# First block's attention: high and low values side by side in one stationary tile, and the taps of each convolution chunk one step later

## What is computed

```python
h = rms_norm(x, mix_norm[l])
z = h @ w_in[l]
q = z[..., :Q_END].reshape(bsz, seq, N_Q_HEADS, HEAD_DIM)      # 8 heads of 64
k = z[..., Q_END:K_END].reshape(bsz, seq, N_KV_HEADS, HEAD_DIM) # 2 heads of 64
v = z[..., K_END:V_END].reshape(bsz, seq, N_KV_HEADS, HEAD_DIM)
attn_out = sliding_window_attention(q, k, v, attn_sink[l])      # blocks of 128, each sees itself and the one before
conv_out = short_conv(z[..., V_END:CB_END], z[..., CB_END:CC_END],
                      z[..., CC_END:CH_END], conv_w[l])         # b * conv3(c * h), causal, per channel
x = x + jnp.concatenate([attn_out, conv_out], axis=-1) @ w_out[l]
```

## Time and profile before

| | before |
|---|---|
| median of 3 runs | 2579.07 us (2578.69 to 2579.18) |
| profiled execution, span | 2577.6 us |
| PE busy | 2559.2 us, 99% |
| DVE busy | 1450.2 us, 56% |
| ACT busy | 947.2 us, 37% |
| POOL busy | 384.2 us, 15% |
| granted TensorE clock, mean | 0.999 of full |

### The profile page before, as it was taken

How to read it: one execution, slowest core, us unless ns; L and a number is a source line. 1 busy time by engine, 2 the same in 40 slices (tenths; PEclk the granted TensorE clock), 3 DMA queues, 4 the chain that set the end, 5 groups by cost and what they waited for, 6 DMA issues and landing times.

```text
span 2577.6 us, 32166 instructions
## 1 busy us (share of the span) xinstructions
PE 2559.2 (99%) x11610; PEld 2120.0 (82%) x11610; DVE 1450.2 (56%) x1735; ACT 947.2 (37%) x1381; POOL 384.2 (15%) x310
## 2 busy tenths in 40 slices
PE   8999999999999999999999999999999999999999
PEld 7888888888888888888888888888888888788887
DVE  7444347764443454443576644434999787642443
ACT  5222234432222232222354322223477534441332
POOL 4000111320001100001123100012177221100001
PEclk9999999999999999999999999999999999999999
DMA  5333332233333333333323333334233333233332
GB/s 160 98 98 94 97 87 83 82 100 96 98 96 96 102 91 97 98 92 98 96 66 91 98 97 98 94 96 126 73 81 76 123 90 112 76 107 97 98 98 82
DMA packets 487838, 247.21 MB, mean 96 GB/s; under 512 B 39874, under 2 KB 484551, under 8 KB 487495
## 3 DMA queue, kind: packets, MB, share of 16 engines
q1 hardware_dynamic: 487298, 245.75, 33.3%
q10 hardware_dynamic: 452, 0.32, 0.1%
HBM read 241.84 MB, written 4.19 MB: 95 GB/s over the span
## 4 chain that ended last, share of the span: by engine, by line
PE 95%; DVE 3%; ACT 1%; issue 0%; DMA 0%; POOL 0%; DVEq 0%; ACTq 0%
PE bank L669 15%; PE bank L668 15%; PE bank L670 15%; PE psT L668 10%; PE psT L669 10%; PE psT L670 10%; PE psS L668 4%; PE psS L669 4%; PE psS L670 4%; PE bank L684 1%; PE bank L677 1%; PE bank L680 0%; PE psT L778 0%; DVE wlo L1755 0%; PE bank L1083 0%; PE bank L1082 0%
## 5 line engine op out<-in xcount | busy, mean ns | idle before, releaser
L1755 DVE TENSOR_TENSOR wlo<-raw,whi 128x1024 fp32r<-128x1024 f32 x466 | 626.3, 1345 | 434.0 <-ACT whi L1285 417.4
L668 PE MATMUL bank<-xhi,whi 128*128 128x512 f32 x1656 | 648.1, 391 | 1.4 <-issue 1.4
L669 PE MATMUL bank<-xlo,whi 128*128 128x512 f32 x1656 | 644.7, 389 | 0.0
L670 PE MATMUL bank<-xhi,wlo 128*128 128x512 f32 x1656 | 644.6, 389 | 0.0
L1285 ACT ACTIVATE whi<-raw 128x1024 fp32r<-128x1024 f32 x463 | 485.3, 1050 | 340.5 <-PE psT L670 316.9
L668 PEld LDWEIGHTS bank<-xhi,whi 128*128 128x128 f32 x1656 | 311.0, 188 | 67.1 <-issue 2.9
L669 PEld LDWEIGHTS bank<-xlo,whi 128*128 128x128 f32 x1656 | 311.0, 188 | 64.7 <-issue 1.4
L670 PEld LDWEIGHTS bank<-xhi,wlo 128*128 128x128 f32 x1656 | 310.8, 188 | 64.9
L668 PE MATMUL psT<-hhi,whi 128*128 128x512 f32 x704 | 273.9, 389 | 0.0
L669 PE MATMUL psT<-hlo,whi 128*128 128x512 f32 x704 | 273.9, 389 | 0.0
L670 PE MATMUL psT<-hhi,wlo 128*128 128x512 f32 x704 | 273.9, 389 | 0.0
(11 more groups left out here) (516 smaller groups left out, 3457.5 us busy)
## 6 DMA issues: line engine op xcount, KB each, us to landing
raw<-in_ffn_wg SPq DMA_DIRECT2D x88, 512.0 KB
raw<-in_ffn_wu SPq DMA_DIRECT2D x88, 512.0 KB
raw<-in_ffn_wd SPq DMA_DIRECT2D x64, 512.0 KB
raw<-in_w_mlp SPq DMA_DIRECT2D x64, 512.0 KB
raw<-in_w_in SPq DMA_DIRECT2D x53, 512.0 KB
raw<-in_ffn_wd SPq DMA_DIRECT2D x32, 384.0 KB
raw<-in_w_in SPq DMA_DIRECT2D x24, 256.0 KB
raw<-in_w_out SPq DMA_DIRECT2D x11, 512.0 KB
```

The costliest lines, as they stand in the source:

```text
L668: pe.matmul(dest, a, rhs_hi(k), start=start and k == 0, stop=False)
L669: pe.matmul(dest, a, rhs_lo(k), start=False, stop=False)
L670: mm = pe.matmul(dest, b_, rhs_hi(k), start=False, stop=stop and k == tiles - 1)
L1755: dve.tensor_tensor(wlo[:, a:a + UNIT], raw[:, a:a + UNIT], whi[:, a:a + UNIT].bitcast(F32), ALU.subtract).then_inc(s_split, 1)
```

## The change

Three things change.

1. `vhi` and `vlo` become one tile `vst` in which each head's 64 high and 64 low columns of v lie side by side. With it as the stationary operand one matmul gives high v x p in rows 0 to 63 of `psO` and low v x p in rows 64 to 127. `pv` makes two matmuls for each key block in place of three (low v x low p comes along).
2. The attention output is the sum of the two halves of `psO`. ACT makes the high part of the first half alone; DVE makes the low part in two operations: first half minus high part into `olow1`, then plus second half.
3. DVE's two taps of chunk i, POOL's gate product and the high and low parts move one step of u later (taps at u = 3i + 4, parts at u = 3i + 5); for the last chunk they stay at u = 12. ACT's first tap stays.

```diff
--- before.py
+++ after.py
@@ -154,13 +154,14 @@
         khh = [sb(f"khh{g}", S, F32R) for g in range(2)]
         kll = [sb(f"kll{g}", S, F32R) for g in range(2)]
         half1 = [slice(0, HD), slice(HD, P)]
-        vhi = sb("vhi", S, F32R)
-        vlo = sb("vlo", S, F32R)
+        vst = sb("vst", 2 * S, F32R)
+        v_part = lambda e: vst[:, :].rearrange("p (n t d) -> p n t d", t=2, d=HD)[:, :, e, :]
         sc = [sb(f"sc{i}", 8 * P) for i in range(2)]
         pthi = sb("pthi", 8 * P, F32R)
         ptlo = sb("ptlo", 8 * P, F32R)
         upad = [sb(f"upad{i}", S + 8) for i in range(2)]
         cy = [sb(f"cy{i}", S) for i in range(2)]
+        olow1 = sb("olow1", S)
         assert at[0] <= top, (at[0] - top)
 
 
@@ -780,18 +781,20 @@
                 mm.then_inc(a_tt, 1)
 
             def pv(l, s):
-                blk = s // 2
+                blk, g = s // 2, s % 2
                 n = 1 if blk == 0 else 2
                 pe.wait_ge(a_th, l * STEPS1 + s + 1)
                 if s:
                     pe.wait_ge(a_ol, l * STEPS1 + s)
-                tiles = [(slice((blk - n + 1 + j) * P, (blk - n + 2 + j) * P), slice(j * 4 * P, (j + 1) * 4 * P)) for j in range(n)]
+                tiles = []
+                for j in range(n):
+                    v0 = (2 * (blk - n + 1 + j) + g) * P
+                    tiles.append((slice(v0, v0 + P), slice(j * 4 * P, (j + 1) * 4 * P)))
                 for j, (vs, ps) in enumerate(tiles):
-                    pe.matmul(psO[:, :], vhi[:, vs], pthi[:, ps], start=j == 0, stop=False)
-                    pe.matmul(psO[:, :], vlo[:, vs], pthi[:, ps], start=False, stop=False)
+                    pe.matmul(psO[:, :], vst[:, vs], pthi[:, ps], start=j == 0, stop=False)
                 pe.wait_ge(a_tl, l * STEPS1 + s + 1)
                 for j, (vs, ps) in enumerate(tiles):
-                    mm = pe.matmul(psO[:, :], vhi[:, vs], ptlo[:, ps], start=False, stop=j == n - 1)
+                    mm = pe.matmul(psO[:, :], vst[:, vs], ptlo[:, ps], start=False, stop=j == n - 1)
                 mm.then_inc(a_pv, 1)
 
             def mix(l, q, N):
@@ -1333,7 +1336,7 @@
                         c += 1
                     if i == 2:
                         act.wait_ge(s_vt, l + 1)
-                        act.activation(vhi[:, :], psT[:, 0:S], ACT.Copy).then_inc(s_vh, 1)
+                        act.activation(v_part(0), psT[:, 0:S].rearrange("p (n d) -> p n d", d=HD), ACT.Copy).then_inc(s_vh, 1)
                     act.wait_ge(s_qs, l * 5 + i + 1)
                     f = tmp[1 + i % 2]
                     if i == 0:
@@ -1354,7 +1357,7 @@
                         act.wait_ge(a_pv, l * STEPS1 + s + 1)
                         rows = slice(g * HD, (g + 1) * HD)
                         act.activation(yhi[rows, 0:4 * S].rearrange("p (c n) -> p c n", c=4)[:, :, blk * P:(blk + 1) * P],
-                                       psO[rows, :].rearrange("p (c n) -> p c n", c=4), ACT.Copy).then_inc(a_oh, 1)
+                                       psO[0:HD, :].rearrange("p (c n) -> p c n", c=4), ACT.Copy).then_inc(a_oh, 1)
                     if 0 <= u - 2 < STEPS1:
                         s = u - 2
                         n = 512 if s < 2 else 1024
@@ -1375,9 +1378,9 @@
                         act.wait_ge(c_u, l * CC + i + 1)
                         act.activation(cy[i % 2][:, :], upad[i % 2][:, 2:2 + S], ACT.Copy,
                                        scale=cw1[:, ds(l * (3 * CC) + 2 * CC + i, 1)]).then_inc(c_t2, 1)
-                    if (u % 3 == 1 and u >= 4) or u == 3 * CC:
-
-                        i = u // 3 - 1
+                    if (u % 3 == 2 and u >= 5) or u == 3 * CC:
+
+                        i = (u - 1) // 3 - (u < 3 * CC)
                         act.wait_ge(c_y, l * CC + i + 1)
                         act.activation(chunk(yhi, 4 + i), cy[i % 2][:, :], ACT.Copy).then_inc(c_yh, 1)
                 for m in range(KC):
@@ -1858,7 +1861,8 @@
                                              inv[:, :], ALU.mult, ALU.mult).then_inc(s_qs, 1)
                     if i == 2:
                         dve.wait_ge(s_vh, l + 1)
-                        dve.tensor_tensor(vlo[:, :], psT[:, 0:S], vhi[:, :].bitcast(F32), ALU.subtract).then_inc(s_vl, 1)
+                        dve.tensor_tensor(v_part(1), psT[:, 0:S].rearrange("p (n d) -> p n d", d=HD), v_part(0).bitcast(F32),
+                                          ALU.subtract).then_inc(s_vl, 1)
                     if i:
                         qk_low(l, i - 1)
                 for i in range(2):
@@ -1890,10 +1894,12 @@
                         dve.wait_ge(a_oh, l * STEPS1 + s + 1)
                         rows = slice(g * HD, (g + 1) * HD)
                         ys = slice(blk * P, (blk + 1) * P)
-                        dve.tensor_tensor(ylo[rows, 0:4 * S].rearrange("p (c n) -> p c n", c=4)[:, :, ys],
-                                          psO[rows, :].rearrange("p (c n) -> p c n", c=4),
-                                          yhi[rows, 0:4 * S].bitcast(F32).rearrange("p (c n) -> p c n", c=4)[:, :, ys],
-                                          ALU.subtract).then_inc(a_ol, 1)
+                        heads = lambda a: a.rearrange("p (c n) -> p c n", c=4)
+                        dve.tensor_tensor(heads(olow1[rows, :]), heads(psO[0:HD, :]), heads(yhi[rows, 0:4 * S].bitcast(F32))[:, :, ys],
+                                          ALU.subtract).then_inc(a_os, 1)
+                        dve.wait_ge(a_os, l * STEPS1 + s + 1)
+                        dve.tensor_tensor(heads(ylo[rows, 0:4 * S])[:, :, ys], heads(psO[HD:P, :]), heads(olow1[rows, :]),
+                                          ALU.add).then_inc(a_ol, 1)
                     if 0 <= u - 2 < STEPS1:
                         s = u - 2
                         n = 512 if s < 2 else 1024
@@ -1924,8 +1930,8 @@
                         c += 1
                     if 4 <= u + 1 < 3 * CC:
                         conv_part(u + 1, q + c)
-                    if u % 3 == 0 and u >= 3:
-                        i = u // 3 - 1
+                    if (u % 3 == 1 and u >= 4) or u == 3 * CC:
+                        i = (u - 1) // 3 - (u < 3 * CC)
                         y = cy[i % 2][:, :]
                         dve.wait_ge(c_t2, l * CC + i + 1)
                         dve.scalar_tensor_tensor(y, upad[i % 2][:, 1:1 + S], cw1[:, ds(l * (3 * CC) + CC + i, 1)], y,
@@ -2202,7 +2208,7 @@
                     rest = olow2[rows, :].rearrange("p (i n) -> p i n", n=P)
                     dve.tensor_tensor(rest, psO[0:HD, 0:2 * P].rearrange("p (i n) -> p i n", n=P),
                                       view(a2h).bitcast(F32), ALU.subtract).then_inc(a_os, 1)
-                    dve.wait_ge(a_os, r + 1)
+                    dve.wait_ge(a_os, L * STEPS1 + r + 1)
                     dve.tensor_tensor(view(a2l), psO[HD:P, 0:2 * P].rearrange("p (i n) -> p i n", n=P), rest,
                                       ALU.add).then_inc(b_ol, 1)
                 if s % 2 == 0 and h < H2:
```

## The result

| | before | changed |
|---|---|---|
| median | 2578.96 us (2578.69 to 2579.34, 21 runs) | 2583.97 us (2581.78 to 2585.82, 21 runs) |
| profiled execution, span | 2577.6 us | 2582.0 us |
| matmuls | 11610 | 11582 |

The account below looks back on a forecast made before the run. TensorE, busy 99% of the span, was taken as the bound, with DVE nearly full in the mixing stage. Per layer -3.17 + 1.7 + 2.5 = +1.0 us, +2.05 us for two layers: 2581.1 us, range 2575.3 to 2584.8.

Parts of the forecast that it names:

- Removed matmuls: Mixing stage on PE: 14 matmuls fewer a layer at 0.2267 us each, 3.17 us a layer, 6.35 us in all.
- The added operation: DVE's second operation for each attention output: 0.73 us more, bounds 0.6 and 0.9 us.
- The steady part: Stretch where scores, softmax and product all run: PE stalls 1.7 us a layer for DVE at step 6's product.
- The walk: DVE's work and waits added up from 433.30 to step 6's low probabilities: 482.07, where PE wants them at 480.36.
- The end of the stage: Output projection's seventh input chunk: PE waits 2.5 us a layer for chunk 2's low part; lower bound 1.2 us.
- the last chunk's cover: Output projection: the last chunk is needed at T + 12.0 and its chain ends near T + 11.1, so no stall.
- the weight splits' lead: Weight splits stand three units ahead of use, some 16 us, so delays of 3 us don't show there.
- the two bare steps: Steps u = 3 and 6, with neither taps nor low part: DVE waits 1.33 us in each, 2.66 us.
- The first: Rival: both stalls absent, all 6.35 us gained, 2572.7 us; 5%.
- the second: Rival: the steady part keeps up and only the end stalls, 2577.7 us; 14%.
- the third: Rival: no exclusion, POOL gets in ahead of the split, the end stalls 1.2 us, 2578.5 us; 14%.
- The fourth: Rival: DVE bounds the steady part, its second operation costing 1.05 us and not 0.73, 2585.0 us; 12%.

Follow-up runs that it names:

- e5: e3 without DVE's second operation, so the attention output lacks v's low values: 2572.69 us, ratio 0.9976.
- e6: e3 with ACT copying the low rows in steps 0 to 5 and DVE adding them for three blocks at once at u = 9: 2572.76 us.
- e7: The changed kernel with DVE's weight split at u = 11 put behind chunk 2's low part: 2580.84 us, ratio 1.0008.
- e2: The kernel before, three products kept, with only the move of the taps and parts: 2587.1 us, ratio 1.0030.
- e3: The changed kernel with chunk 2's taps ahead of the last projection's scaling at u = 10: 2577.16 us, ratio 0.9993.
- e4: The changed kernel with 11 extra matmuls, result unused, ahead of the wait at the output projection's seventh input chunk: 2582.33 us.
- e1: The changed kernel with taps, gate product and convolution parts back at their steps of before: 2581.55 us, ratio 1.0011.

## Why the prediction was right, and where it was off

- **Removed matmuls**, 0.2267 us each, 6.35 us: right; e5 and e6 show 6.1 to 6.2 us. By the 131 ns for a matmul of 512 columns that the Trainium skill gives ("TensorE: Matmul & The Clock Gate", section "Back-to-back issue gap") it would have been 3.7 us; the runs don't bear that out for these matmuls.
- **The added operation**, 0.73 us: the rows of after stand 0.72 and 0.73 us apart, below.

```profile
442.65 0.69 DVE L1898 TENSOR_TENSOR olow<-psO,yhi 64x512 f32<-64x512 f32 x1 [0.85 <-ACT yhi L1359]
443.37 0.69 DVE L1901 TENSOR_TENSOR ylo<-psO,olow 64x512 fp32r<-64x512 f32 x1
444.10 1.23 DVE L1907 TENSOR_TENSOR ptlo<-psT,pthi 128x1024 fp32r<-128x1024 f32 x1
```

- **The steady part**: forecast 1.7 us a layer, measured 2.1. The place and the reason were right (e5). The walk took only the low probabilities as what PE needs; the first of the two pieces waits for `psO`, but the second ends last and sets the time. My walk had DVE at the end of the low probabilities of step 6 at 482.07; in the trace they end at 482.12 (480.89 + 1.23, with the stage 0.18 us earlier), so DVE was 0.2 us later than walked. The remaining 0.2 us was left out of the walk: 0.06 from DVE's end to PE's start at 482.18, and 0.11 because the next PE group follows that pair of matmuls after 0.57 us (482.75) and not 0.46 as before (483.08 to 483.54).
- **The end of the stage**: forecast 2.5 us a layer, measured 2.47 and 0.1 for the restart. Every link held, and so did the exclusion of GpSimd and the vector engine (e7), the last chunk's cover and the weight splits' lead. The step was right because it went by the order of the code at u = 10, and not by the busy shares; e2 and e3 each show it alone.
- **The sum**: forecast +2.05 us, measured +5.0. The median lies in the range, but the change is more than twice the forecast one, and that it stayed below 2584.8 is partly luck: 6 of the 21 runs, those of the upper group, lie above it. What the sum lacked is a term. I had counted PE's idle time at its length, and took the clock for granted, since it was 1.00 in the stage before; but before, PE never waited there. Behind the new waits the clock falls in about half of the stages, 1.6 to 1.8 us each, so about 1.8 us a run on average; e4 takes the idle time away and the fall goes with it. With that term, 0.4 us a layer in the steady part and 0.1 us a layer for the restart at the end the sum is 2.05 + 1.8 + 0.8 + 0.2 = 4.9.
- **Waits that the move takes away**: the 1.23 us at 468.15 did go, but undoing the move costs 0.6 us a layer in the steady part (e1) and not the 2.2 that I expected there. I had added that wait and chunk 1's low part with its wait, and taken nothing off for the 2.66 us that the walk gives the two bare steps, which exist only with the move. How the rest divides was not measured.
- **The rivals**: none of them was the case. The first (all gained) and the second (only the end stalls) are excluded by the waits, the third by the 2.19 us product. The fourth had the right side and nearly the right time (2585.0) for a reason that isn't there: DVE's pair cost 0.73 us.

## What to carry to other kernels

When one engine is busy for all of a stretch, a removed instruction there is worth its distance to the next, and only if no other engine was just keeping up: walk the fullest of them through the stretch with the added work, and see what it must have ready, when. When a piece of work is moved by a step, look at what it now stands behind in its engine's own list; a wait that was harmless at the old place can be the last projection at the new one. An addition that doesn't have to happen at once can be put where the engine waits anyway, which gave here all of what the matmuls were worth.

## What the runs showed of the hardware that was not expected

- TensorE's granted clock fell to 1.2 GHz shortly after a wait of 2.3 us at the end of a stage that was busy before and after it, in about half of the stages; after 1.4 us in few (e7); after 1.26 us with 0.46 us and two matmuls behind it in both layers of the profiled e1; and in none of the 22 stages of e3, with 1.1 and 0.5 us, to judge by its spans (2574.8 to 2575.4). It stayed low for 3.4 us each time that a trace shows it, in the changed kernel with some seven matmuls 0.43 us apart. Why it falls in one of two stages that look alike is open.
- The first matmul after a wait is followed 0.34 us later, at full clock, and not 0.23. Idle time isn't needed for it: in e4, where the 11 matmuls lead up to it and PE's list shows no wait, the distance is 0.33 (502.13 to 502.46). There only the weight load had waited for DVE, 0.28 us.
- A GpSimd product and a vector operation with two inputs from SBUF hold each other up, in both directions: 2.19 us for 1.29, and 1.09 for 0.69. The Trainium skill ("SBUF — State Buffer", section "SBUF: two separate sides") says that whichever starts first has the shared ports for its whole instruction and the other is blocked. The trace agrees but for a small part: POOL ended 1.13 us after the split that held it (500.15 against 499.02) and takes 1.29 alone, and the low part ended 0.55 us after POOL's next product (501.94 against 501.39) and takes 0.69 alone.
